# A decoder layer with 32 routed experts in fp32 on one Trainium2 core: another order of the mixer's first steps, twelve SBUF places for expert weights, and one half of them for each expert

## What is computed

```python
h = layer_norm(x, ln0_g, ln0_b)
proj = h @ w_in                       # qkv, decay and beta, z, the short convolution's xc, gb, gc, qm, 3 gates
km, vm = split(mem @ w_mem_kv)        # 256 memory tokens
y_a = gated DeltaNet(silu(conv4(qkv)), decay, beta) * silu(z)
y_b = gb * conv3(gc * xc)
y_m = softmax(qm km^T / sqrt(128)) vm
mix = (sum over the branches of sigmoid(gate) * (y @ w_br)) @ w_o
h = layer_norm(ALPHA * h + mix, ln1_g, ln1_b)
# top 4 of 32 experts by a softmax router; for each expert, on its tokens:
gate, up = split(h @ w_gate_up[e] + b_gate_up[e])
y = ((clip(up) + 1) * gate * sigmoid(1.702 * gate)) @ w_down[e] + b_down[e]
out = layer_norm(ALPHA * h + sum of weighted y, ln2_g, ln2_b)
```

## Time and profile before

| what | value |
|---|---|
| median of 3 runs | 1277.85 us (1277.75 to 1279.93) |
| the profiled execution, its span from the first to the last instruction | 1278.4 us |
| PE busy | 1215.7 us, 95% of the span |
| DVE, ACT, POOL busy | 394.5, 240.0, 146.1 us |
| moved | 453.62 MB, mean 355 GB/s |
| mean granted TensorE clock | 0.992 of full |

### The profile page before, as it was taken

One profiled execution on the slowest core, in us unless ns is written; L12 is line 12 of the kernel. 1 busy time (PEld: TensorE's weight loads), 2 busy tenths in 40 slices (PEclk: granted clock), 3 DMA queues, 4 the chain that ended last, 5 costly groups with the idle time before them and its releaser, 6 DMA issues.

```text
span 1278.4 us, 16886 instructions
## 1 busy us (share of the span) xinstructions
PE 1215.7 (95%) x7135; PEld 615.8 (48%) x7135; DVE 394.5 (31%) x786; ACT 240.0 (19%) x386; POOL 146.1 (11%) x106
## 2 busy tenths in 40 slices
PE   5999999999999999999999999999999999989996
PEld 5799999998843333333333333333333333323332
DVE  5386553434622211222221221221112222121224
ACT  4364344544310000000000000000000000000001
POOL 8223422455200000000000000000000000000000
PEclk9899999999999999999999999999999999999998
DMA  9533313475799999999999999999999999999994
GB/s 296 204 133 133 132 69 133 186 301 181 296 403 422 427 428 428 387 431 431 431 434 428 428 431 430 431 429 429 429 431 430 434 428 428 432 431 429 427 425 177
DMA packets 49511, 453.62 MB, mean 355 GB/s; under 512 B 6109, under 2 KB 10282, under 8 KB 31018
## 3 DMA queue, kind: packets, MB, share of 16 engines
q1 hardware_dynamic: 49450, 452.71, 85.4%
HBM read 451.64 MB, written 1.05 MB: 354 GB/s over the span
## 4 chain that ended last, share of the span: by engine, by line
PE 71%; DMA 20%; DVE 3%; ACT 2%; POOL 2%; issue 2%; SPq 0%; DVEq 0%; ACTq 0%; POOLq 0%
PE bank L1389 26%; PE bank L1462 13%; DMA late<-in_w_gate_up_dram 11%; DMA raw<-in_w_gate_up_dram 8%; PE bank L1203 6%; PE bank L1204 5%; PE bank L1205 5%; PE bank L1475 4%; PE bank L1360 3%; PE bank L1375 2%; PE bank L1450 1%; ACT late L1175 1%; POOL w_lo L761 1%; ACT w_hi L1080 1%; PE bank L1470 1%
## 5 line engine op out<-in xcount | busy, mean ns | idle before, releaser
L1389 PE MATMUL bank<-late 128*64 128x512 f32 x1664 | 373.6, 596 | 10.4 <-DMA late<-in_w_gate_up_dram 10.4
L1389 PEld LDWEIGHTS bank<-late 128*64 128x64 f32 x1664 | 114.3, 137 | 245.5 <-issue 220.5
L1462 PE MATMUL bank<-late 128*64 128x512 f32 x800 | 178.3, 598 | 4.9 <-ACT late L1175 4.9
L1203 PE MATMUL bank<-act_hi,w_hi 128*128 128x256 f32 x448 | 130.2, 291 | 4.9 <-DVE early L1668 2.6
L1204 PE MATMUL bank<-act_lo,w_hi 128*128 128x256 f32 x448 | 126.5, 282 | 0.0
L1205 PE MATMUL bank<-act_hi,w_lo 128*128 128x256 f32 x448 | 126.4, 282 | 0.0
L1808 DVE TENSOR_SCALAR late<-bank 128x512 f32<-128x512 f32 x32 | 22.1, 691 | 306.7 <-PE bank L1389 306.7
L1462 PEld LDWEIGHTS bank<-late 128*64 128x64 f32 x800 | 55.8, 137 | 110.2 <-issue 102.2
L761 POOL TENSOR_TENSOR w_lo<-raw,w_hi 128x1024 fp32r<-128x1024 f32 x33 | 82.0, 2488 | 114.9 <-ACT w_hi L1080 114.8
L1389 PE MATMUL bank<-raw,late 128*64 128x512 f32 x384 | 86.2, 596 | 4.7 <-DMA raw<-in_w_gate_up_dram 4.7
L1203 PEld LDWEIGHTS bank<-act_hi,w_hi 128*128 128x128 f32 x448 | 85.1, 190 | 7.1 <-DVE early L1668 3.3
(11 more groups left out here) (321 smaller groups left out, 1253.8 us busy)
## 6 DMA issues: line engine op xcount, KB each, us to landing
late<-in_w_gate_up_dram SPq DMA_DIRECT2D x38, 4096.0 KB, 32.0
late<-in_w_down_dram SPq DMA_DIRECT2D x50, 2048.0 KB, 31.3
late<-in_w_gate_up_dram SPq DMA_DIRECT2D x28, 2048.0 KB, 15.5
raw<-in_w_gate_up_dram SPq DMA_DIRECT2D x10, 4096.0 KB, 32.0
raw<-in_w_down_dram SPq DMA_DIRECT2D x14, 2048.0 KB, 26.7
raw<-in_w_in_dram SPq DMA_DIRECT2D x8, 2048.0 KB, 8.1
early<-in_w_in_dram SPq DMA_DIRECT2D x6, 2048.0 KB, 7.8
raw<-in_w_gate_up_dram SPq DMA_DIRECT2D x4, 2048.0 KB, 9.3
```

Source lines behind the costliest of these rows:

```text
L1203: mm(o, l_hi, r_hi, start=start, stop=False)
L1389: ins = mm(bk[64 * c:64 * c + 64, :], x_slotT[:, k % 4, 64 * (k // 4):64 * (k // 4) + 64], w[:, kk, at + 512 * c:at + 512 * (c + 1)], star ...
L1462: ins = mm(ps[3][64 * c:64 * c + 64, :], hidT[:, kk, 64 * q:64 * q + 64], w[:, kk, c * 512:(c + 1) * 512], start=(q == 0 and kk == 0), sto ...
```

## The change

It has three parts. **The mixer's beginning**: SP issues the first piece of slot 0 ahead of the memory tokens, slot 1 ahead of `x` and the layer norm's parameters, and slot 2 ahead of the small tensors. Both layer norm tiles stand after `km`, `vm` stands ahead of all of `hT`, and pieces 9 and 10 behind `hT`. PE starts with ten matmuls on `ident`, and waits for `memT` tiles and `hT` tiles one group of k at a time. ACT loads the table of square roots in its first instruction. `decay_masks()` comes first on POOL, the level masks after piece 8, and the pieces are dealt out to DVE and POOL in another way. **The twelfth place**: `spare`, which the mixer doesn't use, takes chunk 10 (expert 1, chunk 4) right after mixer slot 18. **Halves**: chunk m always lies at place m % 12, so an expert has one half of the ring, chunk m waits for chunk m - 12, all transfers are 2 MB, and `bdown` is loaded with `bgu` during the mixer. To make room, `up1` is gone (the clipped up tile stays in its bank), a few tiny tiles share places, and the program reserves 256 bytes of DMA scratch in each partition (it is not set before).

```diff
-RING = 10
-ROUND = 5
+RING = 2 * EC
+ROUND = 4
+DMA_SCRATCH = 256
...
-    order = [("memT", n) for n in range(3)] + [("prep", 0), ("memT", 3), ("prep", 1), ("prep", 2), ("ln", 0, 0)]
-    order += [("km", 0), ("ln", 0, 1), ("km", 1), ("km", 2), ("cols",), ("km", 3)]
-    order += [("hT", 0, j) for j in range(2)] + [("vm", n) for n in range(NT)] + [("hT", 1, j) for j in range(2)]
-    order += [("qkv", 0), ("qkv", 1), ("ab", 0), ("qkv", 2), ("abT", 0), ("qkv", 3), ("decay functions",)]
+    order = [("prep", 0)] + [("memT", n) for n in range(4)] + [("prep", 1), ("prep", 2)]
+    order += [("km", n) for n in range(4)] + [("ln", 0, t) for t in range(NT)] + [("vm", n) for n in range(NT)]
+    order += [("hT", t, j) for j in range(2) for t in range(NT)] + [("prep", 9), ("cols",), ("prep", 10)]
+    order += [("qkv", 0), ("ab split",), ("qkv", 1), ("ab", 0), ("qkv", 2), ("abT", 0), ("qkv", 3), ("decay functions",)]
...
+    LO_ENGINE[0:12] = ["dve"] * 5 + ["pool"] * 4 + ["dve"] * 3
...
-            r = slot_of(m)
-            fill = MIXER_FILLS[r] + sum(signals(n) for n in range(m + 1) if slot_of(n) == r)
-            per_round = sum(signals(n) for n in range(2 * ROUND * EC, 3 * ROUND * EC) if slot_of(n) == r)
-            return RING_SLOTS[r], RING_IN[r], (rounds * per_round + fill) * 16
+            r = m % RING
+            return RING_SLOTS[r], RING_IN[r], (rounds + (MIXER_FILLS[r] + m // RING + 1)) * 16
...
+                if n == SPARE_AFTER:
+                    chunk_dma(sp, SPARE - EC, w_gate_up[0, 1], w_down[0, 1], *ring_place(SPARE)[0:2])
...
-                if ex == 1 + ROUND:
-                    chunk_spent(sp, WIDE_TO - 1)
-                    for r in range(4):
-                        sp.dma_start(bdown[NE * r:NE * (r + 1), :], b_down[0, :, 512 * (r % 2):512 * (r % 2 + 1)]).then_inc(ebias_in, 16)
-            with sp.Fori(1, ROUNDS - 1) as j:
+                chunk_dma(sp, m - EC, w_gate_up[0, 1], w_down[0, 1], *ring_place(m)[0:2])
+            with sp.Fori(0, (NE - 4) // ROUND) as j:
...
-                    for c in range(0, 4, 2):
-                        m = EC * (2 + ROUND + u) + c
-                        chunk_spent(sp, m + 2 - RING, ROUND * (j - 1))
-                        pair_dma(sp, c, gu, m)
-                    for c in range(4, EC):
-                        m = EC * (2 + ROUND + u) + c
-                        chunk_spent(sp, m + 1 - RING, ROUND * (j - 1))
-                        chunk_dma(sp, c, gu, dn, *ring_place(m)[0:2])
+                    for c in range(EC):
+                        chunk_spent(sp, c, ROUND * j + u)
+                        chunk_dma(sp, c, gu, dn, *ring_place(EC * u + c)[0:2])
...
-            a.copy(ln_std[:, 0:1], eps_ln)
+            a.activation(ln_std[:, 0:1], eps_ln, ACT.Sqrt)
...
+                    if s == ("km", 0) and k % 2 == 0:
+                        wait_copied(pe, "memT", k // 2 + 1)
+                    if s == ("qkv", 0) and k % 4 == 0:
+                        wait_copied(pe, "hT", 2 + k // 2)
...
             pe.wait_ge(consts, 1)
+            keep_warm(10, ps[7])
...
-                d.tensor_scalar(up1, ps[2][:, :], LIMIT, -LIMIT, ALU.min, ALU.max).then_inc(up_cut, 1)
+                d.tensor_scalar(ps[2][:, :], ps[2][:, :], LIMIT, -LIMIT, ALU.min, ALU.max).then_inc(up_cut, 1)
```

More of the change, by code:

```diff
@@ L60 @@
 EC = 6
-RING = 10
-ROUND = 5
-ROUNDS = (NE - 2) // ROUND
+RING = 2 * EC
+ROUND = 4
 TABLES = NE - 10
-assert ROUND * EC % RING == 0 and ROUNDS * ROUND == NE - 2
+assert ROUND % 2 == 0 and (TABLES - 2) % ROUND == 0 and (NE - 4) % ROUND == 0
+DMA_SCRATCH = 256
 LN_EPS = 1e-5
@@ L155, in mixer_schedule @@
             uses[s] = list(range(q, q + n))
-            out += [("prep", m + SPLITS) for m in uses[s] if m + SPLITS < 4 * N_MIX]
+            out += [("prep", m + SPLITS) for m in uses[s] if m + SPLITS < 4 * N_MIX and ("prep", m + SPLITS) not in order]
             q += n
@@ L228, in hybrid_layer @@
         chunk_decay = tiny.new(NPB, 2)
+        ids, cnt, ext, ext2 = tiny.at(ids_o, ITEMS), *(tiny.at(ids_o + ITEMS + n, 1) for n in range(3))
+        assert ids_o + ITEMS + 3 <= tiny.used
         o_ss, o_rs = tiny.new(NPB), tiny.new(NPB)
@@ L288, in hybrid_layer @@
         first_slots = [l.new(SLOT) for _ in range(3)]
-        bgu = l.new(512)
-        gb_cols = l.new(2, KD)
+        bgu, bdown = l.new(512), l.new(512)
         scratch = l.new(2, 1024 - 128)
@@ L294, in hybrid_layer @@
         x_tok = l.new(512)
-        up1, gate1 = l.new(512), l.new(512)
+        gate1 = l.new(512)
         h_tok = gate1
@@ L310, in hybrid_layer @@
         late_slots = [l.new(SLOT) for _ in range(4)]
-        both = l.used - 4 * SLOT
         x1T = l.at(l.used - KD * T, KD, T)
-        assert l.used <= LATE - SLOT, (l.used, LATE)
-        l.used = LATE - SLOT
         once_o = l.used; once = l.new(SLOT)
+        spare = l.new(SLOT)
+        assert l.used == LATE, (l.used, LATE)
+        END = once_o + SLOT
         o = once_o
@@ L405, in hybrid_layer @@
                     piece_end[q] = (bank_full[bank_of(v)], turn_of(v))
-        LO_ENGINE = ["dve" if q < 2 else "pool" if q % 2 == 0 or MIXER_SLOTS[q // 4][0] == "br" else "dve" for q in range(4 * N_MIX)]
+        LO_ENGINE = ["pool" if q % 2 == 0 or MIXER_SLOTS[q // 4][0] == "br" else "dve" for q in range(4 * N_MIX)]
+        LO_ENGINE[0:12] = ["dve"] * 5 + ["pool"] * 4 + ["dve"] * 3
         def lo_engine(q):
@@ L775, in slot_dma @@
             if n == 0:
-                for j in range(4):
-                    sp.dma_start(dst[:, :, j * P:(j + 1) * P], src[:, :, j * P:(j + 1) * P]).then_inc(piece_in[j], 16)
+                sp.dma_start(dst[:, :, j * P:(j + 1) * P], src[:, :, j * P:(j + 1) * P]).then_inc(piece_in[j], 16)
             else:
@@ L846, in bcast @@
                 sp.dma_start(dst, src).then_inc(done, 16)
+            slot_dma(sp, 0, 0)
             sp.dma_start(mem_tok, mem[0].rearrange("(t p) d -> p t d", p=P)).then_inc(mem_in, 16)
-            slot_dma(sp, 0)
+            for j in range(1, 4):
+                slot_dma(sp, 0, j)
+            slot_dma(sp, 1)
             sp.dma_start(hx[:], x[0].rearrange("(t p) d -> p t d", p=P)).then_inc(x_in, 16)
@@ L864, in _ @@
             sp.dma_start(br_bc[:], b_router.broadcast_to([P, NE])).then_inc(router_in, 16)
-            for n in range(2, N_MIX):
+            for n in range(3, N_MIX):
                 slot_dma(sp, n)
@@ L877, in _ @@
                 sp.dma_start(bgu[NE * r:NE * (r + 1), :], b_gate_up[0, :, FF * n + 512 * c:FF * n + 512 * (c + 1)]).then_inc(ebias_in, 16)
+            for r in range(4):
+                sp.dma_start(bdown[NE * r:NE * (r + 1), :], b_down[0, :, 512 * (r % 2):512 * (r % 2 + 1)]).then_inc(ebias_in, 16)
             for n, m in enumerate((ln1_g, ln1_b)):
@@ L1274, in _ @@
                 elif kind == "km":
-                    if s[1] == 0:
-                        wait_copied(pe, "memT", 4)
                     project(s, src_hi, src_lo)
@@ L1301, in _ @@
                 elif kind in ("qkv", "z", "xc", "gc", "gb", "qm", "gate"):
-                    if s == ("qkv", 0):
-                        wait_copied(pe, "hT", 4)
                     project(s, act_hi, act_lo)
@@ L1505, in item @@
                 down(i, places)
-            for i in range(1, 2 * ROUND + 1):
-                item(i, item_places(i))
-            with pe.Fori(2, ROUNDS - 2) as j:
+            item(1, item_places(1))
+            with pe.Fori(0, (TABLES - 2) // ROUND) as j:
                 for u in range(ROUND):
-                    item(ROUND * j + (1 + u), item_places(2 * ROUND + 1 + u, j - 2))
-            for i in range(ROUND * (ROUNDS - 2) + 1, NE - 1):
+                    item(ROUND * j + (2 + u), item_places(2 + u, (ROUND // 2) * j))
+            for i in range(TABLES, NE - 1):
                 item(i, item_places(i), tables=(i == TABLES))
```

102 lines of the change are left out of this document (41 added, 61 removed).

## The result

The changed kernel takes 1269.8 us (median of 4 runs, 1268.7 to 1271.7) against 1277.8 before (4 runs, 1277.7 to 1279.9): a ratio of 0.9935, 95% interval 0.9923 to 0.9947. It is faster by 8.0 us, where the forecast was 15.5 us and its range ended at 1268. The profiled execution took 1270.2 us; its span, from the first instruction to the last, is 1268.5 us.

What follows compares the result with a forecast made beforehand. The stream of expert weights was taken to set the end, mixer savings staying saved. 1278.4 - 9.0 - 4.9 - 3.0 + 3.1 - 1.8 = 1262.8 us profiled, 1262.3 us as median; range 1257.5 to 1268 us.

Steps and rivals of the forecast that it cites:

- The bound: Experts' part: the stream of expert weights sets the end; PE is 1.8 us faster for each expert and waits.
- The ring: Experts' part: extra place, hole, transfer size and PE's earlier start on a chunk together take away 6.6 us.
- the twelfth place: Ring: chunk 10 is loaded in the mixer, so the stream is everywhere one chunk ahead; -4.9 us.
- The size of the transfers: Experts' long paired stretch: 2 MB transfers in place of 4 MB run 0.44% slower; +3.1 us.
- the moment when PE may start: End of the experts: single chunks let PE start without a pair's second half, ending sooner after the last landing; -1.8 us.
- The hole: Stream at 496 to 534 us: the gap at the change from 11 to 10 places goes; -3.0 us.
- The rival of a start that each transfer pays: Experts: 48 more transfers at up to 2.9 us each, 1401 us at full price; chance 0.03.
- That of PE as the limit: Experts: an item grows and PE becomes the limit; at 0.4 us per item 1266.5 us; chance 0.03.
- The beginning: Mixer's start: earlier slots and new order let `("qkv", 0)` start near 41 us, not 49.05; -9 us, bounds -4 and -13.
- the runs' median stands 0.5 us lower than the profile: Last step of the sum: from a profiled execution of 1262.8 us to a median of 1262.3 us.
- the beginning saves 4 us or less: Rival, mixer's start: layer norm holds `vm`'s last quarter and `hT`, PE's clock falls; about 1267.5 us; chance 0.12.
- The signs: Expected in the profile: `("qkv", 0)` near 41 us, 428 GB/s without holes, 8 to 12 us of chunk waits, landing some 50 us.

Runs made afterwards that it cites:

- spare_late: The changed kernel, but the chunk for the ring's extra place is loaded after the mixer, in its turn behind the others; 1275.0 us.
- single_before: The kernel before with every ring transfer a single one of 2 MB, in the old ring of ten places; 1280.5 us, ratio 1.0017.
- ab_early: The changed kernel with the split of the decay weights moved right behind the second layer norm tile, ahead of `vm`; 1263.4 us.
- begin_ab: The kernel before, its ring untouched, with the new mixer's beginning and the decay weights' split moved behind the second layer norm tile; 1273.1 us.
- ring_only: The changed kernel with the old mixer's beginning (order, dealing of pieces, masks, first transfers), so only the ring's changes are left; 1271.7 us.
- piece12_dve: The changed kernel with the low part of the thirteenth piece on DVE in place of POOL, behind the decay weights' split; 1266.1 us.

## Why the prediction was wrong

**The bound: right, but only just.** The stream of weights set the end, and what the ring saved came out in full. Of the 15.1 us of waits for chunks 6.3 are left, all behind 1142 us; had the stream gained that much more, PE would have been the limit.

**The ring, -6.6 us: right in the sum.** From the first gate and up matmul to the end the three profiles of before take 918.0 to 919.5 us, after and its relatives (all but spare_late) 910.0 to 912.2: 911.0 - 918.1 = -7.1 us with the median of the three. Of its terms, the twelfth place (-4.9) measured 5.2 us in time and 4.0 in the experts' part. The size of the transfers (+3.1) measured +3.8, the moment when PE may start (-1.8) measured -1.6, together +2.2 for +1.3. The hole (-3.0) was not undone by itself; it is gone from the windows, and what is left for it and for anything unnamed is -7.1 + 5.2 - 2.2 = -4.1 by the times, and more, -7.1 + 4.0 - 2.7 = -5.8, by the experts' parts (920.8 - 918.1 = 2.7 for single_before). That the terms' errors nearly cancel is partly luck. The rival of a start that each transfer pays is dead at 428 GB/s. That of PE as the limit did not come: an item without a wait starts 27.5 us behind the one before (441.24 and 468.76 in the chain), though PE is now 98% busy in the stretch.

**The beginning, -9 us: wrong, -1.** The steps that the prediction did work out came nearly as said: slot 1 landed at 18.2 us (18.7 forecast), slot 2 at 30.15 (29.5), `vm` waited for piece 7 until 34.5 (35.3), that piece took POOL 2.77 us (2.8 in the sum), `("qkv", 0)` started at 41.7 (41), and the 1 us for a better clock came in the two units behind it: at the place of `("ab", 0)` 8.5 us were won. The step that failed is the next one. The sum took the gain at the start of `("qkv", 0)` for the gain of the kernel, because "whatever the mixer's beginning saves stays saved". But the change moved one more step, `("ab split",)`, which stands in the diff's list of steps behind `("qkv", 0)` and which the prediction never costed. It began 28 us ahead of its use before and had no time in hand after. It cost 4.1 us of wait and 1.5 us of lower clock, 5.6 in all; ab_early gave 6.4 back and begin_ab 5.4.

Two smaller things stand beside it. In these two profiles 1.4 us more were lost behind `("qkv", 2)`: 2.8 us are won there and 1.4 at the first gate and up matmul, since at the output projection the clock fell in after (0.79 over 310 to 318 us) and in the first profile of before did not (1.00). That is the draw of one execution and no work of the change. And the step from profile to median was mis-sized: "the runs' median stands 0.5 us lower than the profile". In the thirteen other profiles the span leaves out 1.7 to 1.8 us of its run's time (1268.5 and 1270.2 for after). So the first span of before, 1278.4 us, stands for a slow execution of about 1280.1, some 2.3 us above the median, and the 0.5 is only what the two differences leave together. A span of 1262.8 us stands for a time of about 1264.5, not 1262.3. With the 5.6 us of `("ab split",)` that makes 1270.1, where 1269.8 was measured; so close a match is partly chance, since the other terms were off by up to 3 us each. That the old `("qkv", 0)` at 49.05 us was late shows too: in the four other profiles with the old beginning it starts at 47.4, 47.5, 48.7 and 48.7 us. With the wait gone the beginning is worth 5.3 us (begin_ab) to 8.3 (ab_early against ring_only); whether the ring makes that difference is not shown, as the intervals of the two overlap.

**The rival "the beginning saves 4 us or less"** comes nearest (1267.5). Part of its mechanism is there: the layer norm did hold the last quarter of `vm`, as ACT rounds piece 7 only behind the second root (30.35 us), and the clock fell (0.76 over 31.8 to 39 us). But the forecast had that wait in it, and `("qkv", 0)` was on time; the loss came from a cause that the rival doesn't name. That the level masks cost nothing on POOL is right in after; that a POOL piece costs DVE something was in the text for piece 7 alone, and it was the next POOL piece but one, beside the cast, that did the harm.

**The signs.** PE's waits for chunks were to be 8 to 12 us and are 6.3; they were to come in many items from about the middle on, and come in the last four experts alone. Landing was to take some 50 us and takes 48.8 at the end, with a median of 36.4 over the whole kernel. 428 GB/s without a hole is there.

What stays open: how the ring's gain divides between the hole and the other terms to within 2 us, and why the clock falls in one execution and not in the next behind the same stop.

## What to carry to other kernels

When a change rewrites the order of a section, list every step whose place among its neighbours changes, short ones too, and ask of each what its engine has in front of it now and who waits for it; a gain read at one marker has to be followed to the next marker that PE passes without waiting. Take the reference for such a marker from several profiles of the kernel before, since one may have caught a low clock. Turn a span into a run's time by the offset between the two, not by one profile's distance from the median. A short DVE cast or an elementwise step on a critical path should not start while GpSimd is in a long elementwise instruction; where it must, give that piece to DVE.

## What was not expected of the hardware

- A DVE cast of 128 x 64 values takes 0.18 us alone and 2.15 us when it starts behind a GpSimd subtraction of 128 x 1024: it waits for that instruction's end (0.04 to 0.05 us before its own in six profiles). The two-input layer norm steps of 128 x 1024 on DVE take 1.28 us alone. Started while such a subtraction runs they took 1.6 to 3.3 us, and each ended 1.1 us behind it (27.29 and 26.21 us, 35.51 and 34.43 in after). Started first, the DVE step keeps its 1.28 us and the GpSimd piece takes 2.77 in place of 2.4.
- The granted clock behind a stop of PE is partly a draw. At or just behind a stop of 4.1 us it fell in four profiles of four, behind one of 3.4 to 3.5 us in seven of eight (not in piece12_dve), behind the one of 2.2 us at the output projection in twelve of fourteen (not in the first of before and not in single_before). The same program differs by up to 1.7 us at one marker between its three profiles, the same beginning by 3.2 us between five.
- 2 MB transfers in a full queue cost 0.4 to 0.5% of the rate of 4 MB ones, and no start of their own, with 48.8 us from issue to landing at the end.
